# Expert matrices in one transfer of 2 MB each, on nine places of 16 KB, in a streaming block with a mixture of experts

## The reference

```python
def hier_moe(x2, w_group, b_group, w_router, b_router, w1, w3, w2):
    ...
    def expert_block(args):
        tok, gte, e = args
        xb = x_pad[tok]
        hb = jax.nn.silu(xb @ w1[e]) * (xb @ w3[e])
        return (hb @ w2[e]) * gte[:, None].astype(x2.dtype)
```

## Time and profile before

| | |
|---|---|
| median of 3 executions | 1102.12 us (1100.73 to 1103.56) |
| the profiled execution | 1105.28 us, span 1103.4 us |
| PE busy | 1008.0 us, 91% |
| VectorE busy | 508.1 us, 46% |
| ScalarE busy | 315.0 us, 29% |
| moved by DMA | 261.22 MB, mean 237 GB/s |
| loads of expert chunks | 192 of 1 MB |

### The profile page before, as it was taken

How to read it: one execution, slowest core, us unless ns; L and a number is a source line. 1 busy time by engine, 2 the same in 40 slices (tenths; PEclk the granted TensorE clock), 3 DMA queues, 4 the chain that set the end, 5 groups by cost and what they waited for, 6 DMA issues and landing times.

```text
span 1103.4 us, 12366 instructions
## 1 busy us (share of the span) xinstructions
PE 1008.0 (91%) x4817; PEld 639.6 (58%) x4817; DVE 508.1 (46%) x918; ACT 315.0 (29%) x584; POOL 36.6 (3%) x51
## 2 busy tenths in 40 slices
PE   4999999999999999999998499999999888999983
PEld 4777866677878879787777244444443333433332
DVE  5235789979536545523325623333332323233334
ACT  6332346555553334533313111111111101001102
POOL 1000000000000000000000100000000000000000
PEclk9999989899999999999998699999999999999997
DMA  6522312111232434512284799999999999999992
GB/s 188 161 77 77 99 54 72 44 39 39 77 114 77 150 118 153 191 39 77 77 297 155 278 422 420 420 421 420 421 420 420 420 422 419 419 422 421 421 417 94
DMA packets 75725, 261.22 MB, mean 237 GB/s; under 512 B 12513, under 2 KB 40210, under 8 KB 51090
## 3 DMA queue, kind: packets, MB, share of 16 engines
q1 hardware_dynamic: 71250, 248.61, 57.7%
q0 software_dynamic: 3104, 7.35, 1.9%
q10 hardware_dynamic: 1312, 4.46, 1.1%
HBM read 260.12 MB, written 4.19 MB: 240 GB/s over the span
## 4 chain that ended last, share of the span: by engine, by line
PE 69%; DMA 16%; DVE 9%; issue 3%; ACT 2%; SPq 1%; ACTq 0%; DVEq 0%
DMA eraw<-in_w 15%; PE ps L1775 14%; PE ps L1513 12%; PE ps L1514 11%; PE ps L1515 11%; PE ps L1800 6%; PE ps L1811 2%; PE ps L1812 2%; PE ps L1675 2%; PE ps L1704 1%; PE ps L1726 1%; PE ps L1654 1%; DVE work L1145 1%; DVE nmax L1165 1%; DVE wlo L1110 1%
## 5 line engine op out<-in xcount | busy, mean ns | idle before, releaser
L1775 PE MATMUL ps<-eraw,XT 128*64 128x512 f32 x1024 | 233.7, 598 | 12.1 <-DMA eraw<-in_w 11.3
L1110 DVE TENSOR_TENSOR wlo<-raw,whi 128x2048 fp32r<-128x2048 f32 (+2 forms) x43 | 95.9, 2230 | 139.7 <-ACT whi L825 139.6
L1775 PEld LDWEIGHTS ps<-eraw,XT 128*64 128x64 f32 x1024 | 70.3, 136 | 142.7 <-issue 137.9
L1800 PE MATMUL ps<-eraw,HT 128*64 128x512 f32 x512 | 114.7, 594 | 13.9 <-issue 13.0
L1513 PE MATMUL ps<-xT_hi,whi 128*128 128x512 f32 (+1 forms) x256 | 106.5, 416 | 0.0
L1514 PE MATMUL ps<-xT_lo,whi 128*128 128x512 f32 (+1 forms) x256 | 101.7, 397 | 0.0
L1515 PE MATMUL ps<-xT_hi,wlo 128*128 128x512 f32 (+1 forms) x256 | 101.7, 397 | 0.0
L1397 DVE TENSOR_TENSOR h<-ps,h 128x512 f32<-128x512 f32 x128 | 79.3, 682 | 44.2 <-PE ps L1812 44.2
L1389 DVE TENSOR_TENSOR Yl<-ps,Yh 128x512 fp32r<-128x512 f32 x32 | 22.1, 691 | 161.4 <-ACT Yh L983 161.4
L825 ACT ACTIVATE whi<-raw 128x2048 fp32r<-128x2048 f32 (+2 forms) x43 | 80.1, 1862 | 56.5 <-PE ps L1515 54.1
L1800 PEld LDWEIGHTS ps<-eraw,HT 128*64 128x64 f32 x512 | 38.8, 137 | 87.6 <-issue 87.5
(11 more groups left out here) (297 smaller groups left out, 1548.5 us busy)
## 6 DMA issues: line engine op xcount, KB each, us to landing
eraw<-in_w SPq DMA_DIRECT2D x192, 1024.0 KB, 27.0
raw<-in_w_in SPq DMA_DIRECT2D x9, 1024.0 KB, 5.2
raw<-in_w_gate SPq DMA_DIRECT2D x8, 1024.0 KB, 5.7
raw<-in_w_ckv SPq DMA_DIRECT2D x8, 1024.0 KB, 5.6
raw<-in_w_out SPq DMA_DIRECT2D x4, 1024.0 KB, 5.0
raw<-in_w_cq SPq DMA_DIRECT2D x4, 1024.0 KB, 5.0
raw<-in_w_co SPq DMA_DIRECT2D x4, 1024.0 KB, 5.0
xrow<-in_x ACTq DMA_DIRECT2D x4, 512.0 KB, 5.0
```

What stands on the lines that cost most here:

```text
L1110: dve.tensor_tensor(wlo[n % 2][:, 0:w], raw[n % RING][:, 0:w], whi[n % 2][:, 0:w].bitcast(f32), ALU.subtract).then_inc(w_lo, 1)
L1775: ins = pe.matmul(ps[1 + c // 2][rows, :], XT[p % 2][:, kk, rows], eraw[W_SLOT[n_]][:, 512 * k:512 * k + 512], start=(kk == 0), stop=(kk = ...
L1800: ins = pe.matmul(ps[4 + n][rows, :], HT[:, ff, rows], eraw[W_SLOT[n_]][:, D * f + 512 * n:D * f + 512 * n + 512], start=(ff == 0), stop=( ...
```

## The change

Each expert matrix is loaded by one transfer of 2 MB, [128, 4096], 16 KB of consecutive rows in each partition. The ring has nine places of 16 KB over the same memory. A pair has six chunks instead of twelve. The rows that belong together are now 8 apart for w1 and w3 and 4 apart for w2, so the transposes read `blk` in steps of 8 columns and `Hs` in steps of 4. On PE all products of w1 stand before `down`, and `down` takes the four hidden tiles of the first half of the columns, then of the second.

```diff
-    E_SLOTS = [R_RAW + 24 * KB, R_A, R_A + 8 * KB, R_RAW + 32 * KB, R_RAW + 40 * KB, R_B, R_B + 8 * KB, R_RAW, R_RAW + 8 * KB,
-               R_RAW + 16 * KB, R_W, R_W + 8 * KB, R_W + 16 * KB, R_W + 24 * KB, R_B + 16 * KB, R_B + 24 * KB,
-               R_A + 16 * KB, R_A + 24 * KB]
+    E_SLOTS = [R_A, R_RAW + 32 * KB, R_B, R_RAW, R_RAW + 16 * KB, R_W, R_W + 16 * KB, R_B + 16 * KB, R_A + 16 * KB]
...
-        for q, c in ((p, 0), (p - 1, 4), (p - 1, 5), (p, 1), (p, 2), (p, 3)):
+        for q, c in ((p, 0), (p - 1, 2), (p, 1)):
...
-        return slice(4 * P * (kk // 4) + kk % 4, 4 * P * (kk // 4 + 1), 4)
+        return slice(kk, D, 8)
...
-            for n in range(7, 7 + RING):
-                sp.wait_ge(w_lo, [c for c in range(NCH) if c % RING == n - 7][-1] + 1)
+            for n, places in ((3, (0, 1)), (4, (2,))):
+                sp.wait_ge(w_lo, [c for c in range(NCH) if c % RING in places][-1] + 1)
                 load_expert(n)
             b, n = use["tm", CH_CO[1], TT - 1]
             sp.wait_ge(bank_full[b], n + 1)
-            for n in range(7 + RING, NS - 2):
+            for n in range(5, NS - 1):
                 load_expert(n)
             sp.wait_ge(xf_stored, 16 * TT)
-            for n in range(NS - 2, NS):
-                load_expert(n)
+            load_expert(NS - 1)
...
-                        if k == 3:
+                        if k == KT - 1:
                             ins.then_inc(e_wused, 1)
...
-                for n, f in [(0, 0), (1, 0), (0, 1), (1, 1)] if c == 4 else [(0, 0), (0, 1), (1, 0), (1, 1)]:
+                for n in (0, 1):
+                    for ff in range(4):
...
-                    up(p, 0, (0, 1))
+                    up(p, 0, range(2))
                     turn_hidden(p - 1)
-                    up(p, 0, (2, 3))
-                    down(p - 1, 4)
-                    down(p - 1, 5)
+                    up(p, 0, range(2, KT))
+                    down(p - 1)
                 else:
-                    up(p, 0)
-                up(p, 1)
+                    up(p, 0, range(KT))
                 if p:
                     combine_half(p - 1, 0)
```

More of the change, by code:

```diff
@@ L619, in _ @@
                     sp.dma_start(rt[:, NG:NG + NE], b_router[0, :].partition_broadcast(P)).then_inc(gain_loaded, 16)
-                    for n in range(3, 7):
+                    for n in (1, 2):
                         load_expert(n)
@@ L663, in _ @@
                     sp.wait_ge(over_pe, i * 5 - (NE * 5 - 1))
-                    for c in range(6):
+                    for c in range(3):
                         sp.dma_start(chunk_view(c, c), expert_src(e, c)).then_inc(over_loaded, 16)
@@ L994, in _ @@
                     output(p - 1)
-                act.wait_ge(e_wused, both_used(p, 1))
+                act.wait_ge(e_wused, both_used(p, 0))
                 if p:
@@ L1414, in body @@
                     add_half(p - 1, 1)
[L1415 removed]
+                dve.wait_ge(e_wused, both_used(p, 1))
                 dve.wait_ge(gg_done, p + 1)
@@ L1763, in transpose_rows, with up @@
                 ins.then_inc(xt_done, 1)
-            def up(p, c, ks=range(4)):
+            def up(p, c, ks):
                 at_ = [W_AT[2 * p + m, c] for m in (0, 1)]
@@ L1771, in up @@
                 for k in ks:
-                    kk = 4 * (c % 2) + k
                     for m, n_ in enumerate(at_):
                         rows = slice(BLK * m, BLK * m + BLK)
-                        ins = pe.matmul(ps[1 + c // 2][rows, :], XT[p % 2][:, kk, rows], eraw[W_SLOT[n_]][:, 512 * k:512 * k + 512],
-                                        start=(kk == 0), stop=(kk == KT - 1))
-                        if k == 3:
+                        ins = pe.matmul(ps[1 + c][rows, :], XT[p % 2][:, k, rows], eraw[W_SLOT[n_]][:, 512 * k:512 * k + 512],
+                                        start=(k == 0), stop=(k == KT - 1))
+                        if k == KT - 1:
                             ins.then_inc(e_wused, 1)
@@ L1786, in turn_hidden, with down @@
                 ins.then_inc(turned, 1)
-            def down(p, c):
-                at_ = [W_AT[2 * p + m, c] for m in (0, 1)]
+            def down(p):
+                at_ = [W_AT[2 * p + m, 2] for m in (0, 1)]
                 for n_ in at_:
@@ L1792, in down @@
                 pe.wait_ge(ht_kept, p + 1)
-                if c == 4 and p:
+                if p:
                     pe.wait_ge(comb_added, NC * p)
-                for n, f in [(0, 0), (1, 0), (0, 1), (1, 1)] if c == 4 else [(0, 0), (0, 1), (1, 0), (1, 1)]:
[L1797 to L1806, removed]
+                for n in (0, 1):
+                    for ff in range(4):
+                        for m, n_ in enumerate(at_):
+                            rows = slice(BLK * m, BLK * m + BLK)
+                            ins = pe.matmul(ps[4 + n][rows, :], HT[:, ff, rows],
+                                            eraw[W_SLOT[n_]][:, D * ff + 512 * n:D * ff + 512 * n + 512],
+                                            start=(ff == 0), stop=(ff == 3))
+                            if (n, ff, m) == (0, 3, 1):
+                                ins.then_inc(y_half, 1)
+                            if (n, ff) == (1, 3):
+                                ins.then_inc(e_wused, 1)
             def combine(t, n, bank):
@@ L1844, in body @@
                     pe.wait_ge(h_done, p)
-                up(p, 2)
+                up(p, 1, range(4))
                 if p:
                     combine_half(p - 1, 1)
-                up(p, 3)
+                up(p, 1, range(4, KT))
             for b in range(8):
@@ L1860, in _ @@
             turn_hidden(NPAIR - 1)
-            down(NPAIR - 1, 4)
-            down(NPAIR - 1, 5)
+            down(NPAIR - 1)
             n_over = pe.value_load(over_i[0:1, 0:1], min_val=0, max_val=MAX_OVER)
@@ L1880, in _ @@
                     pe.wait_ge(over_act, i * 4 - (NE * 4 - 1))
[L1881 to L1885, removed]
+                    for c in (0, 1):
+                        for k in range(KT):
+                            ins = pe.matmul(ps[1 + c][0:BLK, :], XTo[:, k, :], eraw[c][:, 512 * k:512 * k + 512],
+                                            start=(k == 0), stop=(k == KT - 1))
                     ins.then_inc(over_pe, 1)
```

37 lines of the change are left out of this document (16 added, 21 removed).

## The result

| | before | after |
|---|---|---|
| median | 1102.08 us | 1109.43 us (1108.92 to 1110.19, 4 executions) |
| ratio, 95% interval | | 1.0062 (1.0048 to 1.0076) |

The changed kernel is 7.3 us slower by the medians and 6.8 by the ratio; the forecast was 5.9 slower, 1108.0 us. In the changed kernel `load_expert` is L606, the transposes of gathered rows L1753, `up` L1765, `down` L1789, `combine` L1800 and L1801, Yh L974, Yl L1380. These lines of the page answer to the earlier trace rows; the last two are from its part on DMA queues (packets, MB, share), where before had 75725 packets in all and 71250 on this queue.

The account below looks back on a forecast made before the run. From about 634 us the experts' weight transfers, not PE, were taken to set the pace. The terms 3.5 + 1.6 - 4 + 4.8 = +5.9 us, added to the median of 1102.12, gave 1108.0 us; range 1102.5 to 1112.5.

Parts of the forecast that it names:

- part 1: Expert stage's start: first ring place freed after 32 rows instead of 16, delaying every later landing; +3.5 us.
- part 2: Before the expert stage: 16 KB packets slow the `xf` stores, so the last filling load lies beside the first gather; +1.6 us.
- part 3: Full weight stream: 16 KB packets instead of 8 KB save fixed packet cost; -4 us, from 2.3 to 9.7 us saved.
- part 5: Tail: PE work behind the last landing grows from 4.7 to 9.5 us, as landings come in 4 MB blocks; +4.8 us.
- what would make me wrong: Rate up over 1.5%, PE never waiting for weights, or clock staying at half level when the late gather idles PE.
- the slope from 2 to 8 KB: Weight stream: packet cost per KB read from 2 and 8 KB rows; a 16 KB packet saves 3.3 ns.
- the bound: Weight stream: a 16 KB packet at the small packets' slope takes 606 ns and saves 13.9 ns.
- Part 4: PE order in each pair: a 1.65 us wait for Yl behind `down`, period 28.4 us, covered by the stream; no cost.
- Cancelled: Rival: in the stream packets save 9.7 us, at its start the gather hides; -1.4 us, 1100.7 us, chance 0.27.
- No gain in rate: Rival: in the stream, hardware cuts the rows or packets cost by the byte; +9.9 us, 1112.0 us, chance 0.13.
- PE takes over: Rival: PE's own line ends the expert stage if the wait behind `down` is longer; +12 us, 1114.4, chance 0.05.
- Faster: Rival: each transfer in the stream has a fixed cost, so half as many save more; -2.7 us, 1099.4, chance 0.05.

Follow-up runs that it names:

- b0: The changed kernel again, unedited, as yardstick for other runs on its chip; 1109.01 us, 1.0058 of the kernel before.
- b3: The kernel before (1 MB transfers), its first four reloads waiting until four ring places are free; 1106.16 us, 1.0025 of the kernel before.
- a2: The changed kernel with the last load of the ring's first filling issued only after the first gather has landed; 1104.85 us, 1.0010 of the kernel before.
- a3: The changed kernel with the PE order of before: second half of w1's products behind `down`, still 2 MB transfers; 1114.85 us, 1.0110 of the kernel before.
- a4: The changed kernel with the first two reloads of used places cut into 1 MB halves; 1107.68 us, 1.0043 of the kernel before.
- b1: The changed kernel with the last pair alone in 1 MB halves and in the order of before; 1106.96 us, 1.0035 of the kernel before.
- a1: The changed kernel with 8 KB packets, two 8 KB rows per partition in each 2 MB transfer; 1111.47 us, 1.0074 of the kernel before.
- b2: The changed kernel with a2's late load, first reloads of places 0 to 3 in halves, and b1's tail; 1100.37 us, 0.9978 of the kernel before.
- c0: b2 again, unedited, beside c1; 1100.63 us, 0.9981 of the kernel before.
- c1: b2 with the next pair's transposes moved between `down` and `combine`; 1100.54 us, 0.9974 of the kernel before.

## Why the prediction was right, and where its terms were off

The direction and the size hold, 7.3 us against 5.9, but two terms were too small and one thing was not in the sum. Counted from the mark, the last `down` ends 8.6 us later in the changed kernel's profile (+470.9 for +462.3) and 6.6 us later in b0's (+468.9). The first reload's issue, as SP's timeline has it in before, after, b0 and b3, parts this into start, stream and tail:

```profile
631.36 0.81 SPq L608 DMA_DIRECT2D eraw<-in_w  x2
634.98 0.81 SPq L606 DMA_DIRECT2D eraw<-in_w  x2
634.54 0.81 SPq L606 DMA_DIRECT2D eraw<-in_w  x2
631.86 0.81 SPq L608 DMA_DIRECT2D eraw<-in_w  x2
```

These are +9.93, +17.93, +17.70 and +13.40 from the four marks.

| term | forecast | measured |
|---|---|---|
| part 1, first free place | +3.5 | +3.5 by the rows, +2.8 by time (b3) |
| part 2, first gather | +1.6 | +3.0 (6.54 - 3.55); b0 +2.7 |
| slow first rows | not in the sum | +1.5 (8.61 - 7.09); b0 +1.6 |
| part 3, rate | -4 | -6.3 (441.2 for 447.5 us); b0 -6.4 |
| part 5, tail | +4.8 | +5.2 in b0 (10.05 - 4.8), 6.9 in the first profile |

The stream's time is from the first reload's issue to the last landing. For b0: the first reload comes 7.8 us later (17.70 - 9.93), and 7.8 - 6.4 + 5.2 = 6.6, all that is seen. For the first profile: 8.0 - 6.3 + 6.9 = 8.6.

**Part 1** was right. The stream's restart moved from 634 to 638 on the clock, near the 639 I named, but only because the mark came 4.4 us earlier: from the mark the release came 8.0 us later and not 5.1. b3 tests this term alone.

**Part 2** had the right mechanism and too small a size: 3.0 us, near its upper bound of 3.5 and not the middle I took. That packets of the two queues take turns shows in the packets of each queue (count, MB, share) while the stores (q10) ran beside the weights (q1), before from 603 to 614 us and after from 599 to 612:

```profile
q1 hardware_dynamic: 431, 3.14, 67.8%
q10 hardware_dynamic: 422, 1.56, 34.6%
```

```profile
q1 hardware_dynamic: 296, 4.33, 79.4%
q10 hardware_dynamic: 301, 1.10, 20.7%
```

One packet of the stores went for each one of the weights in both kernels, and a packet of weights took 0.31 us before and 0.61 after (medians of the DMA records). The stores went from 8.7 to 12.1 us, and the last load of the filling, which waits for them, was issued 4.8 us later (615.06, 2.0 ahead of the mark; before 614.66, 6.8 ahead; in b0 4.4 later) where I had 3.5. I had the prefetch run out half way through the stores, but with 16 KB packets it stayed beside them: its 6 MB landed at 614.41, the last store at 615.04. So the last 2 MB (615.06 to 623.37) lay beside the gather (616.71 to 623.54) nearly all the way. In the earlier trace rows is the gather's 8.0 us beside a full queue of 8 KB packets; in one of 16 KB the median is 10.4, and that I should have scaled. a2 takes this term and its follower away.

**The clock.** My last sentence on what would make me wrong named the half level, and it came, for the first rows. In the changed kernel, a3, a4, b0 and b1, where the gather is late (transposes at +5.37 to +6.83), the first 32 rows take 8.61 to 10.06 us; in before, a1, a2, b2, b3, c0 and c1, where it is on time (+3.54 to +3.55), 7.09. What PE did ahead of it differs in one thing. Before, it had matmuls in every 1-us window from the mark on, and the granted clock is 0.84 at 627 and 1.00 from 628, as the first rows begin (627.68):

```profile
626.00:627.00 1.00, 0.89 (x5) 0.49 (x3) 0.07 (x1) 0.44 (x2) 0.04 (x1) 0.50 0.00 0
627.00:628.00 1.00, 0.32 (x2) 0.20 (x4) 0.62 (x1) 0.98 (x2) 0.91 (x1) 0.84 0.00 0
628.00:629.00 1.00, 1.00 (x6) 0.29 (x4) 0.00 (x0) 0.83 (x1) 0.32 (x1) 1.00 0.06 16
```

After, it stood idle from 621 to 623 and the full level came at +12 or so from the mark, not +6. The twelve profiles split this way without an exception, though not by the length of the wait: a4, with the shortest (1.6 us), takes 9.14 us for its rows. That the idle time, and not something else that goes with a late gather, holds the clock down is argued from that split and from a2; it was not tried by itself.

**Part 3** had the right sign and too small a size. From the first reload's issue to the last landing it is 441.2 us (634.98 to 1076.20); before, 447.5 (631.36 to 1078.89): 6.3 us, in b0 6.4, and a2 takes 441.2 too. That is 6.4 us / 696 = 9 ns a packet of 16 KB, between the 3.3 by the slope from 2 to 8 KB and the 13.9 by the bound. The failed step is the choice of the nearer slope. The rate rose by 1.4% by these times and by 1.7% by the windows' whole numbers (420 to 427 GB/s); 1.5% was what I had named as what would make me wrong. The misses of parts 2 and 3 have one cause: 16 KB packets made the stream faster and the others' turns longer. But that their sizes nearly cancel (+1.4, +1.5 and -2.3) is luck; nothing in the sum made them equal. The number of transfers gave nothing: 2 MB transfers of 8 KB packets run at 420 GB/s, like those of 1 MB (a1). The completion signals did halve: with 96 transfers fewer, 1536 packets under 512 B are gone, 16 a transfer (12513 before, 10977 after), by which the semaphore of a load rises too; and a1, whose signals halve too, shows no gain in rate from it.

**Part 4** was right: 15 waits of 1.5 us (1.65 forecast), a period of 28.28 (28.4), and no cost. PE begins to wait for w2 at 935 us, not at 806, as forecast. c1 removes 15 us of these waits from b2 and gains nothing; a3 shows what before's order costs with 2 MB places.

**Part 5** was right: 10.05 us behind the last landing in b0 (9.5 forecast), 11.75 in the first profile, where the last `down` ran in part at the half clock (8.78 for 7.09 us), as this window of it shows:

```profile
1081.00:1082.00 1.00, 1.00 (x6) 0.45 (x4) 0.00 (x0) 0.00 (x0) 0.00 (x0) 0.50 0.00 0
```

That is no part of the change: b3, which is the kernel before but for one wait, had 8.78 there too, and c0 and c1 did as well. Ahead of it PE stood idle twice for 0.9 us, for `Hs` and for `HT`; it does so in b0 too, where the clock stayed up. Why some executions have it stays open. b1 gives 2.05 to 2.5 us of the term back by time and 3.1 by the rows.

**The rivals.** "Cancelled" asked for a rate term above 6.6 us, and it came close, 6.4; it fell because it also asked for a hidden gather, and the gather and the slow rows cost 4.5. "No gain in rate" is a1's kernel, which is 8.2 us slower than before by its ratio: parts 1 and 5 alone, 3.5 + 5.2. "PE takes over" did not happen in the changed kernel, though b2 shows the bound one step behind. "Faster" by a fixed cost per transfer falls with a1.

**The filling.** "The same bytes stand behind the same waits" holds from the last dense product on; of the loads ahead of it, 4 MB and not 3 wait for `w_lo` in the changed kernel. Nothing came of it: a1, which has this too, starts its transposes at +3.55 and its reloads at +13.35, where b3 has +13.40.

## What to carry to other kernels

When a stream of loads sets the pace, read its two ends before its rate: the first place that comes free, and the work left behind the last landing. The coarser transfers moved both, by +3.5 and +5.2 us here, against the 6.4 us that the rate gave; keep the large packets, and cut the transfers in halves at the two ends only, which with a gather put ahead of the last prefetch turned +0.6% into -0.2%. And price a larger packet for whoever shares the engines with it: here the stores landed after 12.1 us for 8.7 and the gathers after 10.4 for 8.0.

## What of the hardware was not expected

- The larger packets slowed the other queues. Beside a full queue of 8 KB packets the 512 KB stores landed after 8.6 to 8.7 us and the gathers after 8.0 to 8.3 (medians of before, a1 and b3); beside 16 KB packets after 11.9 to 12.3 and 10.4 to 10.6 (the other nine profiles). The 384 packets of 4 KB of three stores are 8 a store and engine, and 8 more turns' worth of 8 KB at 0.31 us are an estimate of 2.5 us, near the 3.4 (12.1 in b0, 8.7 in a1) and 2.4 (10.4 after, 8.0 before) measured. The DMA records bear out one packet each in turn, beside the counts under part 2. While both queues ran, a weights packet starts within 5 ns of the end of 89% of the store packets before and of 88% after (to 612.5 us); with the times shifted by up to 0.15 us it is 31% and 21%. And store packets, 0.16 us each, follow each other most often after 0.46 us in the kernel before (0.16 + 0.31) and after 0.76 us in the changed one (0.16 + 0.61).
- A cost of each packet still shows at 8 KB: 382, 410, 420 to 423 and 427 GB/s for packets of 1, 2, 8 and 16 KB (after, 900 to 1000 us).
- A wait of 1.6 to 3.1 us for a gather came, in all five profiles that have one, with 1.5 to 3.0 us more in PE's first 32 rows, part of them at the half clock; in the changed kernel the wait cost half as much again.
